# A third PSUM bank for turned attention weights, another order of VectorE's and ScalarE's pieces within a turn, and the first attention's gates on GpSimd

## What is computed

```python
probs = softmax(concat([scores + bias, sink]))[..., :-1]
attn_out = (probs @ v) * silu(attn_gate)              # first block
sc = q @ k * 64 ** -0.5 + bias; p = softmax(sc); o = p @ v      # second block, twice
x = x + (g_a * (o_a @ w_branch_a) + g_b * (o_b @ w_branch_b)) @ w_out
x = x + square(relu(rms_norm(x) @ w_up)) @ w_down
```

## The kernel before

| turn, block i | band: turned | band: quanta | causal: turned | causal: quanta |
|---|---|---|---|---|
| 0, i = 6 | step a=1: 4 | 2, 1, 1 | 4 | 2, 1, 2 |
| 1, i = 7 | step a=1: 3 | 1, 1, 2 | 3 | 1, 1, 2 |
| 2, i = 0 | step a=3: 4, 4 | 0, 1, 0 | 4, 4 | 1, 0, 1 |
| 3, i = 1 | step a=3: 2 | 1, 1, 0 | 4, 3 | 0, 1, 0 |
| 4, i = 4 | step a=0: 3 | 2, 1, 1 | 3 | 1, 1, 2 |
| 5, i = 5 | none | 1, 1, 2 | none | 1, 1, 1 |
| 6, i = 2 | step a=2: 4, 4 | 1, 0, 1 | 4, 4 | 1, 1, 1 |
| 7, i = 3 | step a=2: 2 | 1, 1, 1 | 3 | 1, 0, 1 |

## Time and profile before

### The profile page before, as it was taken

The page is one execution under the profiler, slowest core; times in us unless marked ns, Lnnn a source line. Parts: engine busy times, 40 slices in busy tenths (PEclk is TensorE's granted clock), DMA queues, the critical chain, the costliest instruction groups (busy, mean ns, idle before and its releaser), DMA issues.

```text
span 1980.2 us, 23604 instructions
## 1 busy us (share of the span) xinstructions
PE 1916.1 (97%) x9297; PEld 1586.2 (80%) x9297; DVE 974.4 (49%) x2101; ACT 775.1 (39%) x1482; POOL 68.1 (3%) x133
## 2 busy tenths in 40 slices
PE   8989999999999999999999999999999999999998
PEld 6777788877788777787888888888888888888887
DVE  5788854546666666656512144433333433333234
ACT  5555433346666666667311132221121302112122
POOL 4000001000000000000000000000000000000000
PEclk8999999999999999999999999999999999999999
DMA  5410114322222222212311115121120202112002
GB/s 168 110 33 27 43 55 161 127 56 58 75 65 61 60 60 73 60 53 72 91 54 44 52 47 177 33 74 43 43 64 22 75 32 64 43 43 64 22 22 85
DMA packets 132480, 129.30 MB, mean 65 GB/s; under 512 B 7233, under 2 KB 112265, under 8 KB 132370
## 3 DMA queue, kind: packets, MB, share of 16 engines
q1 hardware_dynamic: 126482, 115.18, 18.9%
q0 software_dynamic: 5888, 12.62, 2.8%
HBM read 105.70 MB, written 15.79 MB: 61 GB/s over the span
## 4 chain that ended last, share of the span: by engine, by line
PE 77%; DVE 10%; ACT 8%; issue 3%; DMA 0%; DVEq 0%; SPq 0%; POOL 0%; POOLq 0%; ACTq 0%
PE b L86 74%; ACT Wf L94 3%; PE b L89 3%; DVE Wf L108 2%; DVE Wr L97 2%; DVE ring L97 1%; ACT Xr L93 1%; ACT ring L93 1%; ACT Wf L93 1%; DVE Xr L97 1%; DVE Xr L105 1%; ACT Wr L93 1%; DVE Wf L97 1%; DVE Wf L105 0%; DVE st L115 0%
## 5 line engine op out<-in xcount | busy, mean ns | idle before, releaser
L86 PE MATMUL b<-Yr,ring 128*128 128x512 f32 x1920 | 511.2, 402 | 1.2 <-DVE Xr L97 1.2
L86 PE MATMUL b<-Xr,ring 128*128 128x512 f32 x1872 | 455.9, 395 | 8.1 <-DVE Wr L97 3.2
L86 PEld LDWEIGHTS b<-Xr,ring 128*128 128x128 f32 x1872 | 347.5, 190 | 76.8 <-issue 7.8
L86 PEld LDWEIGHTS b<-Yr,ring 128*128 128x128 f32 x1920 | 342.0, 190 | 57.0 <-DVE Xr L97 1.8
L86 PE MATMUL b<-Xr,Yr 128*128 128x512 f32 x1104 | 253.9, 390 | 0.0
L86 PEld LDWEIGHTS b<-Xr,Yr 128*128 128x128 f32 x1104 | 206.8, 188 | 42.8
L86 PE MATMUL b<-Yr 128*128 128x512 f32 (+2 forms) x1040 | 236.6, 376 | 0.0
L86 PEld LDWEIGHTS b<-Yr 128*128 128x128 f32 x1040 | 191.1, 188 | 38.3
L94 ACT ACTIVATE Wf<-Wf,st 128x640 f32<-128x640 f32 (+3 forms) x192 | 125.3, 653 | 216.0 <-DVE st L112 78.8
L97 DVE TENSOR_TENSOR Wf<-Wf,b 128x512 f32<-128x512 f32 x144 | 92.6, 683 | 237.1 <-PE b L86 237.1
L93 ACT ACTIVATE Wf<-b 128x512 f32<-128x512 f32 (+3 forms) x215 | 106.0, 493 | 229.2 <-PE b L86 225.6
(11 more groups left out here) (121 smaller groups left out, 1586.0 us busy)
## 6 DMA issues: line engine op xcount, KB each, us to landing
stage<-in_w_in_dram SPq DMA_DIRECT2D x58, 512.0 KB, 3.9
stage<-in_w_up_dram SPq DMA_DIRECT2D x32, 512.0 KB, 3.9
stage<-in_w_down_dram SPq DMA_DIRECT2D x32, 512.0 KB, 3.5
stage<-in_w_out_dram SPq DMA_DIRECT2D x16, 512.0 KB, 3.4
Xr<-Xr POOLq DMA_DIRECT2D x32, 256.0 KB, 3.5
Yf<-in_x_dram SPq DMA_DIRECT2D x8, 512.0 KB, 7.1
Wf<-in_x_dram SPq DMA_DIRECT2D x8, 512.0 KB, 4.5
scratch_x<-Wf SPq DMA_DIRECT2D x8, 512.0 KB, 2.8
```

The lines of the kernel that those rows point to most:

```text
L86: return self.send(lambda e: e.matmul(o, w, a, start=start, stop=stop))
```

## The change

- att: three banks (5, 6, 7) for turned weights in rotation, where there were two. The outputs of all steps go to bank 4 alone; the first products of a step wait for `oadd` of the step before.
- VectorE: `p_low` moves behind the maximum, the shift and (att) `att_out` of the same turn. In swa the normalisation comes right behind `p_low`, then the output; all evacuations of the turn before follow in one go. `split_low` is taken out of the evacuations and done one turn later, at the end of the turn.
- ScalarE: `p_high` comes right behind exp, in att the normalisation behind it; the evacuations of place 0 follow. `split_high` goes to the end of the turn.
- swa: the gate and the low part of the gated output go from VectorE to GpSimd, with the factor 0.5 of the gate now in the copy of the values.

```diff
+ATT_TURN_BANKS, ATT_OUT_BANK = (5, 6, 7), 4
-    def turn_weights(stage, step, g, e_block, rooms):
-        b = TURN_BANKS[turn_count[0] % 2]
+    def turn_weights(stage, step, g, e_block, rooms, banks):
+        b = banks[turn_count[0] % len(banks)]
...
-            pe.wait_ge(*at[freed[b]])
+            pe.wait_ge(*at[room_free])
...
-                     [("v", step.pair, h) for h in range(2)], m.pt2, 0, b)
+                     [("v", step.pair, h) for h in range(2)], m.pt2, 0, ATT_OUT_BANK,
+                     ("oadd", "att", step.n - 1) if step.n else freed[ATT_OUT_BANK])
```

```diff
 # scalar_program, att (in swa alike; out_high also moves behind place 0's evacuations)
             act.activation(e, e, FN.Exp, ...)
-        att_ended(("att", t, 0))
         for step, g in turn.turned:
             p_high("att", step, g, m.pt2)
         if turn.slot is not None:
             act.activation(e, e, FN.Copy, scale=stats[:, 0, 4:5])
+        att_ended(("att", t, 0))
         att_ended(("att", t, 1))
...
         att_ended(("att", t, 2))
+        att_split(t)
```

```diff
 # vector_program, att
     for t, turn in enumerate(att):
-        for step, g in turn.applied:
-            p_low("att", step, g, m.pt2)
         if turn.slot is not None:
...
         for step, g in (att[t - 1].applied if t > 0 else ()):
             if g == len(step.groups) - 1:
-                att_out(dve, m, at, note, step)
-        if t:
-            att_ended(t - 1, (0,))
+                att_out(dve, m, at, step)
+        for step, g in turn.applied:
+            p_low("att", step, g, m.pt2)
         if turn.slot is not None:
             one_over("att", s, 3)
         if t:
-            att_ended(t - 1, (1, 2))
+            att_ended(t - 1, (0, 1, 2))
+        if t > 1:
+            att_split(t - 2)
```

```diff
 # gpsimd_program
+    def swa_gate(n):
+        p, i = n // 8, n % 8
+        c0 = (i % 4 - 1) * P
+        pool.wait_ge(*at["oadd", "swa", n])
+        pool.wait_ge(*at["free", f"ag{p}", i // 4])
+        pool.tensor_tensor(m.och1, m.och1, m.sg[note.sg[f"ag{p}", i // 4]][:, c0:c0 + 256], ALU.mult).then_inc(
+            m.g_b, ("ogated", n))
+        y, c = m.Y[4 + p], slice((i - 1) * P, (i + 1) * P)
+        pool.wait_ge(*at["ohigh", n])
+        pool.tensor_tensor(y[:, 1, c], m.och1, f32(y[:, 0, c]), ALU.subtract).then_inc(m.g_b, ("olow", "swa", n))
```

More of the change, by code:

```diff
@@ L930, in tensor_program @@
             ring.prepare(place[0], 1)
+    freed[ATT_OUT_BANK] = ("oadd", "att", 63)
     place[0] = ("att", len(att), 0)
@@ L1137, in swa_ended, with swa_split, out_high @@
                 evac_gate(name, h)
-        split_high(place)
+    def swa_split(t):
+        for x in range(3):
+            split_high(("swa", t, x))
+    def out_high(n):
+        c = slice((n % 8 - 1) * P, (n % 8 + 1) * P)
+        act.wait_ge(*at["ogated", n])
+        act.wait_ge(*at["ext saved"])
+        act.activation(m.Y[4 + n // 8][:, 0, c], m.och1, FN.Copy).then_inc(m.a_hi, ("ohigh", n))
     def evac_gate(name, h):
@@ L1153, in scalar_program @@
     swa_ended(("swa", -1, 0))
+    swa_split(-1)
     for t, turn in enumerate(swa):
@@ L1164, in scalar_program @@
             act.activation(stats[:, 0:2, 6], stats[:, 0:2, 5], FN.Exp).then_inc(m.a_exp, ("exp", "swa", s.n))
+        for step, g in turn.turned:
+            p_high("swa", step, g, m.pt1)
+        swa_ended(("swa", t, 0))
         for step, g in (swa[t - 2].applied if t > 1 else ()):
             if step.n % 2:
[L1167 to L1173, removed]
+                out_high(step.n)
         swa_ended(("swa", t, 1))
@@ L1315, in att_ended, with att_split @@
                     evac_v(name, m.vT2, h, ("vturned", n - 1, 1) if h == 0 else ("vturned", n, 0))
-        split_high(place)
+    def att_split(t):
+        for x in range(3):
+            split_high(("att", t, x))
     def evac_th(name, h):
@@ L1638, in vector_program @@
     swa_ended(-1, (0, 1, 2))
+    swa_split(-1)
     for t, turn in enumerate(swa):
-        for step, g in turn.applied:
-            p_low("swa", step, g, m.pt1)
         if turn.slot is not None:
@@ L1871, in vector_program @@
     att_ended(-1, (0, 1, 2))
+    att_split(-1)
     for t, turn in enumerate(att):
-        for step, g in turn.applied:
-            p_low("att", step, g, m.pt2)
         if turn.slot is not None:
@@ L2086, in att_out @@
     dve.wait_ge(*at["ostored", step.n - 2] if step.n > 1 else (None, 0))
-    dve.tensor_tensor(r[own, :], m.banks[note.bank["o", "att", step.n]][own, 0:256], m.tmp2[own, :], ALU.add).then_inc(
+    dve.tensor_tensor(r[own, :], m.banks[ATT_OUT_BANK][own, 0:256], m.tmp2[own, :], ALU.add).then_inc(
         m.v_o, ("oadd", "att", step.n))
@@ L2156, in gpsimd_program @@
                     k_dup("k", m.k1, h)
+        for step, g in (swa[t - 1].applied if 0 < t <= len(swa) else ()):
+            if step.n % 2:
+                swa_gate(step.n)
     for stage, slot, t in (("y", 1, 0), ("y", 1, 1), ("c", 2, 0), ("y", 1, 2), ("c", 2, 1), ("c", 2, 2)):
```

69 lines of the change are left out of this document (30 added, 39 removed).

## The result

The changed kernel takes 1990.74 us (median of 4 runs, 1990.36 to 1991.37) where the kernel before takes 1980.84: ratio 1.005, interval 1.0032 to 1.0067. It is 9.9 us slower; the forecast was 30. The profiled execution has a span of 1988.3 us, 8.1 more than before, and that is what the traces can explain.

A forecast was written before the change was run, and what follows sets the result against it. PE, busy 97% of the span, was taken as the bound, so only its waits mattered. 1981.9 + 31 (att) - 1 (swa) = 2012, less 1.1 for the median of the runs: 2011 us, range 1983 to 2032.

The forecast's parts named there:

- They cancel: Rival, 6%: new waits of 35 to 40 us in att offset what is taken away, 1981 us.
- What the change takes away: Att: 29.0 us of transposes' waits for `p_low` and 5.1 us of clock falls in pairs 4 to 6, together -34 us.
- The rule of the Trainium skill that I had weighed as a rival: Rival, 15%: PE's frequent short idles in att make its clock fall eight to twelve times, 1.7 us each, 2028 us.
- The new waits in att: Products wait for the later `p_low`: 2.4 us per band head, 4.2 per causal head, eight of each, 19 and 34 us.
- Att: 19 + 34 + 2 + 10: Att's added waits: band heads, causal heads, pair 7's fewer quanta, late evacuations and splits; less 34 removed, +31 us.
- turn 5 of a band head: Att: PE reaches the products 2.05 us after the scores, `p_low` is done at 2.85, a new wait of 0.8 us.
- The fourth group's bank: Causal turn 3 in att: the fourth group needs the first group's bank, a wait of 1.74 us in every causal head.
- The late evacuation: Att: an evacuation ending a short turn delays the maximum: 1.4 us over turn 7's 0.35 per band pair, 0.75 per causal pair.
- Moved DMAs: none is moved in a queue ... so this is hidden: SP's next weight load waits a turn (4 us) longer for `split_low`, hidden by pieces of about four turns, two staged ahead.
- `split_low`'s move: Att: the split, moved a turn later into turn 2, makes VectorE late by 0.45 us in each band pair.
- Swa: Swa: 12 us of old idle time taken away and 11 us of new waits put back, -1 us, bounds -10 to +8.
- the gates: Swa: moving gates and low parts to GpSimd takes 13 us off VectorE, an engine that is not the bound.

The follow-up runs named there:

- a_split_mixed: The changed kernel with VectorE's low half of att's weight splits one turn late, as before, from pair 7 on only: 1982.24 us, ratio 1.0005.
- b_split_mixed: The kernel before with only att's `split_low` moved to the end of a turn, two turns late in pairs 0 to 6, one in pair 7: 1960.03 us.
- a_split_early: The changed kernel with VectorE's low half of att's weight splits one turn late again, not two, in all turns: 1993.87 us, ratio 1.0063.
- a_gates_dve_last: The changed kernel with swa's gates and low parts back on VectorE, behind the turn's evacuations: 1994.46 us, ratio 1.0064.
- b_gates_pool: The kernel before with only swa's 16 gates and 16 low parts moved to GpSimd (factor 0.5 in v's evacuation): 1983.72 us, ratio 1.0009.

## Why the prediction was right in sign and wrong in size

- **The sign: luck.** The change comes out slower only by the late load in pair 7, which the forecast put at nothing. In a_split_mixed, where that load is early again and all else is as changed, the time is that of the kernel before (1.0005, 0.9996 to 1.0013). That is the rival "They cancel", to which I gave 6%: its new waits of 35 to 40 us are what the traces give without the load, some 34 in pairs 0 to 6 and 6 in pair 7.
- **What the change takes away: right.** All 29.0 us of transposes' old waits are gone, and so are the falls of the clock in pairs 4 to 6 (0.97 to 1.00 between 700 and 900 us). The rule of the Trainium skill that I had weighed as a rival (TensorE: Matmul & The Clock Gate, "A second HAM failure mode: psum-queue depth-cycling"), that frequent short idles of PE make its clock swing, does not show here: there are 45 waits at products, and no swing in att outside pair 7's long one.
- **The new waits in att: right in kind and place, about 1.6 times too large.** This is the mis-sized term that made the sum too large ("Att: 19 + 34 + 2 + 10"). In turn 5 of a band head I had 0.8 us; the changed kernel shows 0.39 in its list and 0.54 from start to start:

```profile
571.72 0.76 PE L86 MATMUL b<-Xr 128*128 128x384 f32 x4
...
573.22 0.15 DVE L112 TENSOR_REDUCE st<-st 128x1 f32<-128x2 f32 x1
573.30 0.42 DVE L97 TENSOR_TENSOR Wf<-b,Wf 64x256 f32<-64x256 f32 x1
...
573.64 0.54 DVE L97 TENSOR_TENSOR Wr<-b,Wr 128x384 fp32r<-128x384 f32 x1
```

  I added durations of rows, but `p_low` starts 0.34 us behind `att_out`, whose row is 0.42 long: VectorE's next instruction starts some 0.08 before the last one's row ends, and so it does behind the shift. The products start 2.52 us after the scores (574.24 - 571.72), not 2.85. Waits of 0.35 to 0.8 us are differences of two such sums, and lose a third to a half by that. Per pair (the same matmul in pair after pair) I had 6.65 us of new waits in the band and 9.15 in the causal pairs; the traces give 3.65 (587.67 - 526.11 = 61.56 before, 61.29 after, plus the 3.9 removed) and 6.3 (68.69 before, 69.42 after, plus 3.9 and the 1.7 of the clock). Over pairs 0 to 6 that is 54 against 34 us.
- **The fourth group's bank: right in kind, smaller in size.** It is the 9.9 us of 8 waits at L89, one in each causal head; seven of 1.2 to 1.5 us and one of 0.7, where I had 1.74 (13.9 in all):

```profile
725.13 1.27 DVE L97 TENSOR_TENSOR Wr<-b,Wr 128x512 fp32r<-128x512 f32 x2
...
725.86 0.55 PE L89 MATMUL b<-identf,Wf 128*128 128x128 f32 x3 [1.21 <-DVE Wr L97]
```

- **The late evacuation: wrong in size.** Behind 578.58 I had 1.75 us; it is 0.52 (0.7 from start to start). I let the maximum start behind an evacuation that itself had kept its old start, but the reciprocal ahead of it comes earlier now: 2.19 us after the scores of its turn (578.38 - 576.19), where it came after 3.28 (585.31 - 582.03). Of these 1.09 us, 0.75 are the moved split again: in b_split_mixed, where only that is moved, it is 2.53 (578.73 - 576.20). In the kernel before the split stood ahead of the `p_low` and the maximum of the turn before (the row at 578.22, of before); the other rows are of after:

```profile
578.22 1.22 DVE L97 TENSOR_TENSOR ring<-stage,ring 128x1024 fp32r<-128x1024 f32 x1
```

```profile
578.58 1.39 DVE L105 SCALAR_TENSOR_TENSOR Xr<-b,Xr 64x512 fp32r<-64x512 f32 x2
...
580.82 1.29 DVE L97 TENSOR_TENSOR Wr<-b,Wr 128x512 fp32r<-128x512 f32 x2
...
581.56 1.34 PE L86 MATMUL b<-Wr,Xr 128*128 128x256 f32 x8 [0.52 <-DVE Wr L97]
```

- **"Moved DMAs: none is moved in a queue ... so this is hidden": a second step that failed, the other way.** It holds in pairs 0 to 6, where the delay is even a gain. In pair 7 a piece is prepared in every turn, so two pieces staged ahead are two turns ahead, not eight. It costs 8.5 to 9.3 us (a_split_mixed). The forecast named the price ("a turn per piece would be lost") and a wait for weights among the signs of being wrong, and did not look at the stretch where a piece lasts a turn.
- **The same step missed a gain.** I priced `split_low`'s move at a loss of 0.45 us in a band pair. a_split_early shows a gain of 12.3 us in pairs 0 to 6. On the kernel before, b_split_mixed shows that the old place made half of the earlier trace rows, and was worth 21.5 us with the clock and the short waits. A list of waits names the instruction that PE waited for, `p_low`; what had delayed that one was the row ahead of it.
- **Swa: right in sign, for two reasons that I had not separated.** Swa's stretch gained 3.0 us (139.48 against 142.52) where I had 1. With the gates on VectorE ahead of the evacuations the new order costs 8.1 us and GpSimd's gates gain 11.1; with them behind, it is 1.0 and 4.1. I had costed the gates at nothing, as work of an engine that is not the bound; a_gates_dve_last shows 6.5 us for their place ahead of evacuations.
- **The size of the sum.** Att came to +12.2 us (532.21 - 519.97, from the table) where I had +31. Pairs 0 to 6 came to -0.9 (454.13 against 455.06) where my terms give +22.4: 20 us less of new waits, and 1.7 for a fall of the clock near att's start that I had not counted (0.99 before and 1.00 after over pairs 0 to 3); under 2 us stay unexplained. Pair 7 came to +13.2 where they give +8.7: some 5 less of new waits, 9.3 more from the late load.

## What to carry to other kernels

An engine's slack is a matter of places, not of sums: look at the row just ahead of the instruction that a wait names, and move that one before buying another buffer. A piece of work that frees a buffer belongs to a transfer's loop; count its delay where that loop is shortest, not where it is usual. A list of waits leaves out the short ones: before a difference is put down to something else, compare the starts of the same instructions in both traces. When several edits hang on one semaphore, price them in pairs: the third bank was worth 39 us with `p_low` last, 6.6 alone, and nothing or less with `p_low` in front and the split late.

## What the runs showed of the hardware

While GpSimd works, some of VectorE's instructions stand still. In b_gates_pool's timeline two normalisations take 1.10 us where GpSimd's operation of 106.67 runs, and 0.62 (111.09) where none does; the two-column sum takes 0.55 beside it and 0.17 alone:

```profile
106.32 0.17 DVE L97 TENSOR_TENSOR st<-st 128x2 f32<-128x2 f32 x1 [1.06 <-ACT st L93]
...
106.67 0.74 POOL L97 TENSOR_TENSOR Yr<-Wf,Yr 128x256 fp32r<-128x256 f32 x1 [6.63 <-ACT Yr L93]
106.73 1.10 DVE L101 TENSOR_SCALAR Wf<-Wf,st 128x256 f32<-128x256 f32 x2
...
110.09 0.74 POOL L97 TENSOR_TENSOR Wf<-Wf 128x256 f32<-128x256 f32 x1 [2.67 <-DVE Wf L97]
110.30 0.55 DVE L97 TENSOR_TENSOR st<-st 128x2 f32<-128x2 f32 x1 [0.29 <-ACT st L93]
...
111.09 0.62 DVE L101 TENSOR_SCALAR Wf<-Wf,st 128x256 f32<-128x256 f32 x2
```

The sum ends with GpSimd's row (110.85 and 110.83). Maxima, which read the bank, take 419 ns on the mean in the changed kernel, where a quarter of them run beside a GpSimd operation, and 417 before. So a small operation can lose as much as a large one, and what counts is not how many columns the two engines share but whether a short one on the critical path meets a long one. The Trainium skill has this in SBUF — State Buffer, "SBUF: two separate sides": the pair of ports that the two engines share is held by one instruction at a time, and the other waits in full. The trace agrees.
